# Cross-partition scales of a hybrid layer made by TensorE and VectorE instead of GpSimd's all-reduce

## The reference

```
mod = silu(c) @ W_ada + b_ada                      # six vectors of 1024: shift, scale, gate, twice
h   = RMSNorm(x) * (1 + sc) + sh
z   = h @ W_in                                     # q | k | v | g | low rank | u
GLA : two scans of gated linear attention (4 heads), sum, RMSNorm per head, * silu(g)
FNet: real part of a 2-D DFT over positions and channels of u
y   = concat(GLA, FNet) @ W_out ;  x += gate * RMSNorm(y)
h   = RMSNorm(x) * (1 + sc) + sh
x  += gate * RMSNorm(relu(h @ W1)^2 @ W2)          # W1 1024 x 4096, W2 4096 x 1024
```

## Time and profile before

| what | us |
|---|---|
| median of 3 runs | 1484.57 |
| lowest, highest | 1483.46, 1489.77 |
| span of the profiled execution, first to last instruction | 1476.2 |
| PE busy in the span | 1252.9 (85%) |
| DVE, ACT, POOL busy | 747.0, 425.2, 256.6 |

### The profile page before, as it was taken

One profiled execution on the slowest core, in us unless ns is written; L12 is line 12 of the kernel. 1 busy time (PEld: TensorE's weight loads), 2 busy tenths in 40 slices (PEclk: granted clock), 3 DMA queues, 4 the chain that ended last, 5 costly groups with the idle time before them and its releaser, 6 DMA issues.

```text
span 1476.2 us, 18755 instructions
## 1 busy us (share of the span) xinstructions
PE 1252.9 (85%) x7319; PEld 736.4 (50%) x7319; DVE 747.0 (51%) x1093; ACT 425.2 (29%) x736; POOL 256.6 (17%) x416
## 2 busy tenths in 40 slices
PE   3449999999862338976879999999999999999995
PEld 2225568886651314433445454454554545546442
DVE  3364583892652434755545444444545354454537
ACT  4354352322111215643333032130311312213103
POOL 1111120430212111112211111202112111121104
PEclk9779999999785768988989999999999999999998
DMA  9822011434300220000011110101011010111003
GB/s 294 266 92 63 29 58 37 147 112 147 118 29 0 105 109 29 1 14 16 29 57 34 54 57 30 58 30 57 32 55 58 29 57 29 58 39 48 29 0 128
DMA packets 70751, 97.24 MB, mean 66 GB/s; under 512 B 3077, under 2 KB 53386, under 8 KB 70666
## 3 DMA queue, kind: packets, MB, share of 16 engines
q1 hardware_dynamic: 70666, 96.04, 19.9%
HBM read 86.33 MB, written 9.70 MB: 65 GB/s over the span
## 4 chain that ended last, share of the span: by engine, by line
PE 47%; issue 2%; DVE 1%; POOL 1%; ACT 1%; POOLq 0%; ACTq 0%; DVEq 0%
PE bank L1202 47%; ACT bank L866 1%; POOL region L833 1%; DVE region L2055 0%; POOL small L757 0%; DVE region L2026 0%; POOL small L677 0%; DVE region L1953 0%; DVE ghb L1953 0%; ACT whi L554 0%; DVE region L2057 0%; DVE region L1942 0%; POOL small L755 0%; ACT region L1115 0%; ACT region L1120 0%
## 5 line engine op out<-in xcount | busy, mean ns | idle before, releaser
L1202 PE MATMUL bank<-region,whi 128*128 128x384 f16 (+1 forms) x1872 | 460.4, 328 | 47.8 <-issue 31.9
L1202 PE MATMUL bank<-whi,region 128*128 128x512 f16 (+1 forms) x1872 | 487.9, 348 | 8.9 <-DVE region L1909 8.9
L1202 PE MATMUL bank<-wlo,region 128*128 128x512 f16 (+1 forms) x936 | 325.3, 348 | 0.0
L1202 PE MATMUL bank<-region,wlo 128*128 128x384 f16 (+1 forms) x936 | 307.2, 328 | 0.0
L1202 PEld LDWEIGHTS bank<-region,whi 128*128 128x128 f16 (+1 forms) x1872 | 183.3, 98 | 174.5 <-issue 37.8
L1202 PEld LDWEIGHTS bank<-whi,region 128*128 128x128 f16 x1872 | 184.2, 98 | 170.5 <-DVE region L1909 9.8
L1202 PE MATMUL bank<-region 128*128 128x512 f16 (+8 forms) x802 | 176.0, 386 | 64.0 <-DVE region L1858 34.3
L2026 DVE SCALAR_TENSOR_TENSOR region<-bank,small,region 128x512 f32<-128x512 f32 x144 | 106.7, 749 | 180.5 <-PE bank L1202 180.1
L554 ACT ACTIVATE whi<-stage,small 128x2048 f16<-128x2048 f32 (+1 forms) x42 | 82.3, 1960 | 338.3 <-PE bank L1202 291.1
L1202 PEld LDWEIGHTS bank<-region 128*128 128x128 f16 (+4 forms) x802 | 112.7, 171 | 119.5 <-issue 48.2
L702 POOL PARTITION_ALL_REDUCE small<-small x45 | 76.3, 1695 | 407.1 <-DVE small L537 335.1
(11 more groups left out here) (152 smaller groups left out, 900.7 us busy)
## 6 DMA issues: line engine op xcount, KB each, us to landing
stage<-in_w_fc SPq DMA_DIRECT2D x32, 1024.0 KB, 5.2
stage<-in_w_ada SPq DMA_DIRECT2D x16, 1024.0 KB, 5.3
region<-in_w_ada SPq DMA_DIRECT2D x8, 1024.0 KB, 12.0
stage<-in_w_in SPq DMA_DIRECT2D x8, 1024.0 KB, 5.4
x_with_position<-region SPq DMA_DIRECT2D x9, 512.0 KB, 4.9
region<-x_with_position SPq DMA_DIRECT2D x9, 512.0 KB, 9.1
out_dram<-region SPq DMA_DIRECT2D x9, 512.0 KB, 2.6
region<-in_x_sample SPq DMA_DIRECT2D x8, 512.0 KB, 10.6
```

The source lines that it names most:

```text
L1202: return nc.tensor.matmul(out, lhsT, rhs, start=start, stop=stop, skip_group_check=True)
```

## The change

All scales that are used ahead of the feed-forward loop are made without POOL. The reduction over partitions takes one of two forms.

- A sum: PE multiplies a 128 x 128 matrix of ones by the column of partition maxima, so that every partition gets the sum of the 128 maxima, which is an upper bound of the maximum. DVE copies the column out of PSUM and makes scale and factor (`totals`, `chunk_scale`, `chunk_factor`, `y_scale`). This is used for the nine W_in chunks, the four W_out chunks, both halves of y and `h_scale(0)`.
- A transposed maximum: PE transposes the column into a row (`max_rows`), DVE takes its maximum and spreads it on a small diagonal (`max_of_rows`), PE multiplies by ones (`max_spread`), DVE copies. This is used for `h_scale(1)` and the first two chunks of W1.

The reductions inside the feed-forward loop stay on POOL, from the third W1 chunk on. The new matmuls take banks of ring B, at places set by hand in `b_keys`. Cut to its core:

```diff
@@ ring B
+            if n == 5:
+                b_keys.append(("sum", 0))
+    b_keys.append(("hsum", 0))
...
+        if s == 4:
+            b_keys += [("sums", 4), ("maxT", 0)]
+        if s == 5:
+            b_keys.append(("max", 0))
+        if s == 7:
+            b_keys.append(("sum", len(zin) + 2))
+    b_keys += [("oT", b_order[-1]), ("ysum", 0)]
...
+        if j in (6, 7):
+            b_keys.append(("max", j - 5))
+        if j in (5, 6):
+            b_keys.append(("maxT", j - 4))
@@ POOL
-            h_scale(0)
-            for i in range(1, len(zin)):
-                chunk_scale(i)
...
-                if s == 6:
-                    y_scale(1)
-                if s == 8:
-                    chunk_scale(len(zin) + 2, False)
-                if s == 4:
-                    h_scale(1)
-                    chunk_scale(len(zin), False)
-                    chunk_scale(len(zin) + 1, False)
...
-            y_scale(0)
-            for c in range(3):
-                chunk_factor(len(zin) + c)
-            chunk_scale(len(zin) + 3, False)
-            chunk_factor(len(zin) + 3, s_cof)
+            pool.wait_ge(s_hsc, 2)
...
-                if s in (5, 6):
-                    ff_up_scale(0, s - 5)
+                if s in (8, 9):
+                    ff_up_scale(0, s - 8)
@@ ACT
-                if j == 6:
+                if j == 7:
                     chunk_high(act, ff_split)
@@ PE
+            def total(key, src, ready, count):
+                pe.wait_ge(ready, count)
+                bank = B.open(pe, key)
+                mm(bank[:, 0:src.shape[-1]], ones, src, True, True).then_inc(B.filled(key), 1)
...
+            total(("hsum", 0), hmx[0][:, 1:3], s_hmx, 2)
...
+                if i + 2 < len(zin):
+                    chunk_total(i + 2)
...
+                if s == 4:
+                    pe.wait_ge(s_ymx, 1)
+                    pe.wait_ge(s_wmax, len(zin) + 2)
+                    key, c = ("sums", 4), len(zin) % 8
+                    bank = B.open(pe, key)
+                    mm(bank[:, 0:1], ones, ymx[:, 1:2], True, True)
+                    mm(bank[:, 1:3], ones, wmax[:, c:c + 2], True, True).then_inc(B.filled(key), 1)
+                    max_rows(0, hmx[1][:, 1:3], s_hmx, 4)
+                if s == 5:
+                    max_spread(0, 2)
+                if s == 7:
+                    chunk_total(len(zin) + 2)
             turn_o(NT - 1, b_order[-1])
+            total(("ysum", 0), ymx[:, 0:1], s_ymx, 2)
...
+                    if c == 0 and j == 0:
+                        chunk_total(len(zin) + 3)
...
+                if j in (6, 7):
+                    max_spread(j - 5, 1)
+                if j in (5, 6):
+                    i = ff_split + j - 5
+                    max_rows(j - 4, wmax[:, i % 8:i % 8 + 1], s_wmax, i + 1)
@@ DVE
+            def totals(key, n):
+                bank = B.take(dve, key)
+                V.tensor_copy(tot[:, 0:n], bank[:, 0:n]).then_inc(B.read(key), 1)
+                B.wait_read(dve, key)
+            def max_of_rows(q, n):
+                key = ("maxT", q)
+                bank = B.take(dve, key)
+                V.tensor_reduce(mxv[0:n, :], bank[0:n, 0:P], AX_X, ALU.max).then_inc(B.read(key), 1)
+                B.wait_read(dve, key)
+                V.tensor_scalar(mxd[0:n, 0:n], ident[0:n, 0:n], mxv[0:n, :], None, ALU.mult).then_inc(s_mxd, 1)
+            def chunk_scale(i, at=0):
+                c = slice(i % 8, i % 8 + 1)
+                step(V.tensor_scalar(winv[:, c], tot[:, at:at + 1], 1.0 / TOP, TINY, ALU.mult, ALU.max))
+                V.reciprocal(wscl[:, c], winv[:, c]).then_inc(s_wscl, 1)
...
             for i in range(G_A):
+                if i >= 1:
+                    totals(("sum", i + 1), 1)
+                    chunk_scale(i + 1)
+                    step(chunk_factor(i + 1))
                 chunk_max(dve, i + 2)
...
+            totals(("sum", G_B), 1)
+            chunk_scale(G_B)
+            step(chunk_factor(G_B))
             step(V.memset(Srf, 0.0))
...
+                if s == 5:
+                    totals(("sums", 4), 3)
+                    max_of_rows(0, 2)
+                    y_scale(1, 0)
+                    chunk_scale(w0, 1)
+                    chunk_scale(w0 + 1, 2)
+                    own.did(chunk_factor(w0))
                 if s + 1 < NT:
                     scores(s + 1, b_order[s + 1])
...
                 if s == 6:
+                    totals(("max", 0), 2)
+                    h_scale(1)
+                    scale_gains(1)
                     chunk_max(dve, w0 + 2)
...
+            totals(("ysum", 0), 1)
+            y_scale(0)
+            chunk_factor(w0 + 1).then_inc(s_cof, 1)
             low_y(0, (1,))
             chunk_max(dve, w0 + 3)
             low_y(0, (0,))
             chunk_low(dve, w0 + 2)
+            totals(("sum", w0 + 3), 1)
+            chunk_scale(w0 + 3)
+            step(chunk_factor(w0 + 3))
...
             for j in range(NT + 2):
+                if j in (7, 8):
+                    totals(("max", j - 6), 1)
+                    chunk_scale(F + j - 7)
+                if j in (6, 7):
+                    max_of_rows(j - 5, 1)
...
-                if j == 6:
+                if j == 7:
                     chunk_low(dve, F)
```

More of the change, by code:

```diff
@@ L162, in hybrid_step @@
         a_keys += z_uses(i)
-    b_keys += [("la", d, k, t) for k in range(HK) for d in range(2) for t in range(TB)]
+        if i == LR:
+            b_keys.append(("sum", 1))
+        if i in (Q, U_A):
+            b_keys += [("la", d, int(i == U_A), t) for d in range(2) for t in range(TB)]
+        if i + 2 < len(zin):
+            b_keys.append(("sum", i + 2))
     f_order = [0] + list(range(1, NT))
@@ L288, in hybrid_step @@
         hgo = cols(1)
+        tot = cols(3)
+        mxv, mxd = cols(1), cols(2)
         neg = cols(5)
@@ L1253, in ada_rows, with max_rows, max_spread, chunk_total @@
                         mod_out(len(ada1) + m, ada2[m])
+            def total(key, src, ready, count):
+                pe.wait_ge(ready, count)
+                bank = B.open(pe, key)
+                mm(bank[:, 0:src.shape[-1]], ones, src, True, True).then_inc(B.filled(key), 1)
+            def max_rows(q, src, ready, count):
+                pe.wait_ge(ready, count)
+                key, n = ("maxT", q), src.shape[-1]
+                bank = B.open(pe, key)
+                mm(bank[0:n, 0:P], src, ident, True, True).then_inc(B.filled(key), 1)
+            def max_spread(q, n):
+                key = ("max", q)
+                pe.wait_ge(s_mxd, q + 1)
+                bank = B.open(pe, key)
+                mm(bank[:, 0:n], ones[0:n, :], mxd[0:n, 0:n], True, True).then_inc(B.filled(key), 1)
+            def chunk_total(i):
+                total(("sum", i), wmax[:, i % 8:i % 8 + 1], s_wmax, i + 1)
             def turn(key, src, ready):
@@ L1314, in _ @@
                     ins.then_inc(A.filled(key), 1)
+                    if i == LR and n == 0:
+                        chunk_total(1)
                 if i == Q:
@@ L1578, in finish_gains, with h_scale, chunk_factor, y_scale @@
                 V.tensor_reduce(hmx[norm][:, 2:3], shf[norm], AX_X, ALU.max, apply_absolute_value=True).then_inc(s_hmx, 1)
+            def totals(key, n):
[8 more added lines that the diff above has]
+                V.tensor_scalar(mxd[0:n, 0:n], ident[0:n, 0:n], mxv[0:n, :], None, ALU.mult).then_inc(s_mxd, 1)
+            def h_scale(n):
+                step(V.tensor_tensor(hmx[n][:, 0:1], tot[:, 0:1], tot[:, 1:2], ALU.add))
+                step(V.tensor_scalar(hinv[n], hmx[n][:, 0:1], D ** 0.5 / TOP, TINY, ALU.mult, ALU.max))
+                V.reciprocal(hscl[n], hinv[n]).then_inc(s_hsc, 1)
+            def chunk_scale(i, at=0):
+                c = slice(i % 8, i % 8 + 1)
+                step(V.tensor_scalar(winv[:, c], tot[:, at:at + 1], 1.0 / TOP, TINY, ALU.mult, ALU.max))
+                V.reciprocal(wscl[:, c], winv[:, c]).then_inc(s_wscl, 1)
+            def chunk_factor(i):
+                c = slice(i % 8, i % 8 + 1)
+                if i < len(zin):
+                    other, factor = hinv[0], DK ** -0.5 if i == Q else 1.0
+                else:
+                    half = wout[i - len(zin)][1]
+                    other, factor = yinv[:, half:half + 1], 1.0
+                return V.tensor_scalar(wcof[:, c], winv[:, c], other, factor, ALU.mult, ALU.mult)
+            def y_scale(half, at=0):
+                p = slice(half, half + 1)
+                step(V.tensor_scalar(yinv[:, p], tot[:, at:at + 1], 1.0 / TOP, TINY, ALU.mult, ALU.max))
+                V.reciprocal(yscl[:, p], yinv[:, p]).then_inc(s_ysc, 1)
             def scale_gains(norm):
@@ L1652, in _ @@
                     chunk_max(dve, 1)
+            totals(("sum", 1), 1)
+            chunk_scale(1)
+            step(chunk_factor(1))
             def decay_bias(k):
@@ L1899, in _ @@
                     chunk_low(dve, w0 + 1)
+                if s == 8:
```

(3 more changed lines are left out.)

57 lines of the change are left out of this document (19 added, 38 removed).

## The result

The kernel after took 1387.16 us (median of 4 runs, 1386.93 to 1395.45), the kernel before 1484.68 in the same session. The ratio is 0.935, with a 95% interval of 0.932 to 0.938: 6.5% faster. The prediction's sum was 1386.2. The profiled execution of after took 1386.93 us with a span of 1384.0, 92.2 less than the span of before, where the prediction had 98.4 less.

The account below looks back on a forecast made before the run. POOL's reductions, queued ahead of others' work, were taken to bound the kernel before the feed-forward loop. Terms -20.7 + 1.4 + 1.7 - 60.9 - 19.9 = -98.4 took span 1476.2 to 1377.8, plus 8.4 gives 1386.2 us; range 1368 to 1410.

Parts of the forecast that it names:

- The likeliest case: Whole kernel: the forecast itself, 1386.2 us with its own range 1374 to 1398, chance 0.61.
- start: Before W_in: ACT begins h 20.2 us earlier without POOL's reductions, chunk 1's scale saves 0.5 more; -20.7 us.
- W_in chunks: W_in: seven more small PE matmuls of 0.2 us each, +1.4; the scale work on DVE and ACT stays hidden.
- gate stage: Gate stage: DVE clears Srf only after the last chunk's sum, so the first silu_gate starts later; +1.7 us.
- attention, to the first W_out tile: Attention blocks 4 to 8: without POOL's reductions the first W_out tile comes at 485.8 instead of 528.51; -42.7 us.
- first W_out tile to the last of block 0: W_out block 0: DVE's steps replace POOL's y scale and chunk reduction, 12.1 us instead of 30.3.
- rest of W_out: W_out blocks: post's waits for POOL go, -22.2, against +2.3 for added maxima and moved casts; -19.9 us.
- behind it: After W_out: the wait before the second half of the first up product stays, no change; 0 us.
- The prediction's chain: Attention from outputs(4): step-by-step times, output to gate_o 4.3 us, from 432.3 to the first W_out tile at 485.8.
- Rival 1: Attention and first W_out tiles: PE keeps full clock and DVE's steps overlap better; 1373 us, chance 0.17.
- waits of over 3 us on ring B in several blocks: Attention: a stated sign of being wrong, PE waiting over 3 us for PSUM banks of ring B in several blocks.
- the 8.9 us: First up product: PE's wait before its second half, from POOL's memset and third W1 chunk reduction, expected to stay.

Follow-up runs that it names:

- The kernel with POOL's two reductions: The kernel after, with the scales of the first two W1 chunks back on POOL at W_out blocks 5 and 6; 1402.69 us, ratio 0.945.
- that with only the new start: The kernel before, with only the scales of the nine W_in chunks and the first h made by PE sums; 1462.27 us, ratio 0.984.
- the kernel with midway sums: The kernel after, with W_in chunk sums placed behind the first tile of the next chunk; 1391.19 us, ratio 0.939 without the two longest.
- the kernel with three unused reductions: The kernel after, with three POOL reductions on constants added at attention block 4, results unread; 1424.75 us, ratio 0.958.

## Why the prediction was right, and where it wasn't

The likeliest case came, 1387.2 against 1386.2. By its terms, from the two profiles:

| term | predicted, us | after less before, us |
|---|---|---|
| load phase | 0 | +5.5 |
| start | -20.7 | -20.7 |
| W_in chunks | +1.4 | -1.0 (first chunk) and +8.0 |
| gate stage | +1.7 | +1.0 |
| Fourier stage | 0 | +0.7 |
| attention, to the first W_out tile | -42.7 | -38.5 |
| first W_out tile to the last of block 0 | -18.2 | -19.1 |
| rest of W_out | -19.9 | -22.8 |
| behind it | 0 | -5.5 |
| sum, of the spans | -98.4 | -92.3 |

**That it came within 1 us is partly luck.** Attention gave 4.2 us less than predicted, and W_out 3.8 and the stages behind it 5.5 more. The load phase and the clock in W_in cost some 13 us that the terms don't have, and the 8.4 us that the prediction added between the span of before and the median took up most of them. Of the 8.4 some 2 to 3 lie outside the span (2.9 in after's own execution); the rest says that the profiled execution of before was a quick one.

**Start: right**, in size and in cause. The gap is 8.34 to 8.36 us in all ten profiles of kernels with the new start, and 29.01 and 26.92 in the two of before.

**W_in: right in substance, and the row of the table misleads.** Nearly all of the 8.0 (7.8 from Q chunk to V_A) is the granted clock of that execution: before has 111.1 us too when it falls. In executions without a fall at the logits the chunks with sums took 104.4 and 102.6 us, against 103.2. So a sum costs PE about 0.2 us, as the term had it.

**Gate stage: right in cause, a little too large.** The clearing costs 1.04 us, not 1.7, and goes when it is moved.

**Attention: the step that was mis-sized.** Blocks 0 to 3 gave 2.6 us that I hadn't counted (PE waited 0.95 us for a load of a modulation chunk, before 3.60), and from block 4 on it was 35.9, not 42.7. The prediction's chain begins at the end of `outputs(4)`; from there on it was 34.4. Against that chain:

- `gate_o` of block 4 was taken to end 4.3 us behind its output, by ACT's squares and POOL's root. It ended 5.6 behind it (421.9 to 427.5), since DVE was in its own queue until 426.42, with two `chunk_max` ahead, 4.47 us. The wait of 5.2 us for the sums was 6.04.
- The three bank waits that follow from the prediction's times are there (for the transposition of `scores(7)`, for `turn_o(5)` and for the last one; 3.51, 5.01 and 4.54 us), and a fourth, of 3.80, ahead of the last output.
- The largest part is PE's own work. From `scores(6)` to `outputs(8)` the large matmuls took 8.14, 8.56, 7.22 and 4.50 us, 28.4 in all, where the prediction has 7.3, 6.8, 5.7 and 3.5, 23.3 in all. Its prices for outputs lie between the rows of before at the half and at the full clock, and those for scores are near the full clock.

Rival 1, that shorter gaps give the clock back, didn't come: the granted clock rose from 0.66 to 0.75 over the stretch shown above, but PE was busy longer in it, not shorter. That mean counts the waits too, and says little of the clock at which the matmuls ran.

The prediction named waits of over 3 us on ring B in several blocks as a sign of being wrong. There are four. Three of them follow from its own times, so the sign contradicted its chain; the fourth is the miss. Two of its sums are also off: the pieces listed up to the last tile of block 0 make 12.95, not 12.1, and those of rival 1 make 16, not 13.

**W_out: right.** `post` came every 12.7 us (nine from 508.4 to 610.2), predicted 12.5. The wait of about 3 us for the bank ahead of the transposed maximum is there, 3.27. The kernel with POOL's two reductions prices the W1 part at 19.9.

**Behind it:** the 8.9 us stayed, 9.16. Of the 5.5 us less, 2.1 lie ahead of the first down tile, where kernels with the same code there differ by more (110.7 to 114.2 us). The other 3.4 do go with the change: from the first down tile to the end it is 673.0 us in both profiles of before, and 669.6 to 670.3 in all ten of edited kernels, that with only the new start among them. Both profiles of before have two PE gaps there, 2.9 and 2.8 us together, marked "issue" and in the same places, 530 and 341 us ahead of the end; none of the ten has them. The term was put at 0 because the loop isn't edited. Why the gaps go stays open.

The rule on PSUM in the Trainium skill (GPSIMD Engine Reference, section 3.2: TensorE's way across partitions goes through PSUM) bears on this stage. The trace agrees, by the four bank waits. Where the prediction names the rule, it lets it weigh 5.2 and about 1 us. The 5.2 is a wait for DVE's maximum and not for a bank, and the bank waits in its own chain (445.5 to 449.8, 456.6 to 461.7, 475.9 to 481.0) are far more than 1. With the sums in ring A and read earlier, the stage was 17 us shorter, so the price was too low.

## What to carry to other kernels

A cross-partition reduction on POOL is dear by what stands behind it in POOL's queue: here it was 13 to 14 us for each (in before one of them, ahead of the root of s = 8, took 18.0), less what the waiting engine's own queue hides. Small results that go through a ring of PSUM banks turn the ring for all keys that follow, so put them in a ring whose banks are freed at once, and read them ahead of the long step, not behind it (here both were done together). Look at two profiles of the kernel before: here two executions of one kernel differ by 13 us in span, more than most terms of such a sum.

## What the hardware showed that I had not expected

The same stretch of full PE work runs at a different clock from one execution to the next. From Q chunk to V_A, with PE busy in all of it, the granted clock was 0.99, 0.91, 0.92, 0.98 and 1.00 in five profiles, and the time 103.2, 111.1, 111.0, 104.4 and 102.4 us. The 0.99 and 0.98 come from a short fall at the start of Q chunk. The first twelve logit matmuls, which use 32 rows, took 4.13 us in four of the twelve profiles, at 2.4 GHz, and 4.78 to 5.40 in the other eight, partly at 1.2. In all these eight the fall begins while they run, with a sum behind them or not. In the Fourier stage the same shows: 45.5 to 57.3 us for the same instructions, at 1.00 to 0.79. These are the stretches of the kernel with midway sums and of after:

```profile
307.50:364.80 57.30, 55.08 (x323) 40.63 (x321) 16.21 (x51) 13.20 (x28) 4.42 (x5) 0.79 0.40 129
```

```profile
317.80:364.10 46.30, 44.08 (x323) 32.82 (x321) 16.26 (x51) 13.15 (x28) 4.42 (x5) 1.00 0.49 160
```

What decides it was not found. The edits don't: after and the kernel with three unused reductions have the same code up to there, and took 46.3 and 55.4 us.
